# RMS norms by token sums, small roots and a spread by TensorE, early table loads, and a new order in the first head

## What is computed

```python
def rmsnorm(x, g):                      # first block: EPS 1e-6
    xf = x.astype(jnp.float32)
    y = xf * lax.rsqrt(jnp.mean(xf * xf, axis=-1, keepdims=True) + RMS_EPS)
    return (y * g.astype(jnp.float32)).astype(x.dtype)
...
for l in range(DEPTH):                  # DEPTH = 2
    h = h + hybrid_mixer(rmsnorm(h, norm_mix[l]), ...)
    h = h + expert_choice_ffn(rmsnorm(h, norm_ffn[l]), ...)
return rmsnorm(h, norm_final)
...
x = x + sincos_2d(x.shape[1])           # second block
sh1, sc1, gt1, sh2, sc2, gt2 = adaln(c, ada_w[l], ada_b[l])
hx = modulate(rms_norm(x, norm1_g[l]), sh1, sc1)
x_mix = token_mixer(hx @ w_in[l], ...)  # its readout norms each head's 128 values
x = x + gt1 * x_mix
x = x + gt2 * hier_moe(modulate(rms_norm(x, norm2_g[l]), sh2, sc2), ...)
return rms_norm(x, final_norm_g)
```

## Time and profile before

| | |
|---|---|
| three runs | 2255.35, 2257.14, 2259.73 us; median 2257.14 |
| profiled execution | 2259.7 us; its span in the profile 2257.8 us |
| TensorE matmul busy | 1972.8 us, 87% of the span |
| TensorE weight loads busy | 1197.8 us, 53% |
| VectorE busy | 660.3 us, 29% |
| ScalarE busy | 553.7 us, 25% |
| DMA | 748.76 MB, 332 GB/s over the span |

### The profile page before, as it was taken

The page is one execution under the profiler, slowest core; times in us unless marked ns, Lnnn a source line. Parts: engine busy times, 40 slices in busy tenths (PEclk is TensorE's granted clock), DMA queues, the critical chain, the costliest instruction groups (busy, mean ns, idle before and its releaser), DMA issues.

```text
span 2257.8 us, 29187 instructions
## 1 busy us (share of the span) xinstructions
PE 1972.8 (87%) x12802; PEld 1197.8 (53%) x12802; DVE 660.3 (29%) x1074; ACT 553.7 (25%) x849; POOL 0.2 (0%) x4
## 2 busy tenths in 40 slices
PE   7989998777787999998798889879999998888886
PEld 7978943122131897893333434338989843333332
DVE  3477510000000447750150111036657400000001
ACT  3457300000000346630021221023444311010101
POOL 0000000000000000000000000000000000000000
PEclk9999999999999999998999999999999999999999
DMA  9722789999999963378999999983423899999996
GB/s 362 269 105 95 310 356 422 421 421 422 421 421 420 367 241 115 122 310 354 421 418 413 400 418 417 421 327 113 149 94 129 363 422 422 422 422 422 422 422 274
DMA packets 153247, 748.76 MB, mean 332 GB/s; under 512 B 6064, under 2 KB 18608, under 8 KB 78768
## 3 DMA queue, kind: packets, MB, share of 16 engines
q1 hardware_dynamic: 153136, 747.11, 82.4%
HBM read 746.04 MB, written 1.05 MB: 331 GB/s over the span
## 4 chain that ended last, share of the span: by engine, by line
PE 55%; DMA 33%; DVE 5%; ACT 4%; SPq 2%; issue 1%; DVEq 0%; ACTq 0%
PE bank L724 19%; DMA ring<-w_expert_up 11%; DMA ring<-w_expert_down 11%; PE bank L790 9%; DMA ring<-moe_w_down 6%; PE bank L820 5%; PE bank L752 5%; PE bank L727 5%; DMA arena<-moe_w_down 4%; PE bank L831 3%; SPq L2808 2%; PE bank L974 1%; PE bank L994 1%; PE bank L735 1%; PE bank L1041 1%
## 5 line engine op out<-in xcount | busy, mean ns | idle before, releaser
L790 PE MATMUL bank<-ring,arena 128*32 128x512 f32 x2560 | 484.0, 599 | 81.9 <-DMA ring<-w_expert_up 49.3
L820 PE MATMUL bank<-ring,arena 128*32 128x512 f32 x1280 | 286.5, 608 | 80.7 <-DMA ring<-w_expert_down 60.7
L790 PEld LDWEIGHTS bank<-ring,arena 128*32 128x32 f32 x2560 | 122.4, 110 | 400.2 <-issue 255.8
L724 PE MATMUL bank<-arena_parts,ring_parts 128*128 128x256 f32 x1376 | 314.3, 283 | 2.3 <-DVE ring_parts L2453 1.6
L724 PEld LDWEIGHTS bank<-arena_parts,ring_parts 128*128 128x128 f32 x1376 | 233.4, 189 | 11.7 <-issue 3.1
L820 PEld LDWEIGHTS bank<-ring,arena 128*32 128x32 f32 x1280 | 67.9, 111 | 287.9 <-issue 155.1
L1519 ACT ACTIVATE arena<-bank 128x512 f32<-128x512 f32 (+1 forms) x150 | 76.0, 536 | 515.5 <-PE bank L806 241.1
L2035 DVE TENSOR_TENSOR arena<-arena,bank 128x512 f32<-128x512 f32 x24 | 15.8, 685 | 594.4 <-PE bank L790 594.4
L724 PE MATMUL bank<-ring_parts 128*128 128x256 f32 x768 | 153.7, 290 | 10.0 <-DVE ring_parts L2453 5.3
L724 PE MATMUL bank<-hnT_parts,ring_parts 128*128 128x256 f32 x544 | 155.3, 285 | 0.0
L752 PEld LDWEIGHTS bank<-arena 128*128 128x128 f32 x512 | 124.6, 334 | 20.8 <-issue 20.5
(11 more groups left out here) (353 smaller groups left out, 2362.1 us busy)
## 6 DMA issues: line engine op xcount, KB each, us to landing
ring<-w_expert_down SPq DMA_DIRECT2D x64, 2048.0 KB, 26.1
ring<-w_expert_up SPq DMA_DIRECT2D x60, 2048.0 KB, 23.8
ring<-w_expert_gate SPq DMA_DIRECT2D x56, 2048.0 KB, 23.7
ring<-w_in SPq DMA_DIRECT2D x34, 2048.0 KB, 11.2
ring<-moe_w_up SPq DMA_DIRECT2D x24, 2048.0 KB, 28.8
ring<-moe_w_gate SPq DMA_DIRECT2D x20, 2048.0 KB, 32.4
ring<-moe_w_down SPq DMA_DIRECT2D x16, 2048.0 KB, 32.7
arena<-moe_w_down SPq DMA_DIRECT2D x16, 2048.0 KB, 32.1
```

The source lines that it names most:

```text
L724: last = pe.matmul(out[:, n * S:(n + 1) * S], w[:, k, n * P:(n + 1) * P], x[:, k, :], start=first, stop=final)
L790: last = pe.matmul(banks[bank0 + f][32 * e:32 * e + 32, :], x_slots[:, c, 32 * e:32 * e + 32], w[:, k, i, f * 512:(f + 1) * 512], start=c ...
L820: last = pe.matmul(banks[4 + d][32 * e:32 * e + 32, :], hidT[:, f, 32 * e:32 * e + 32], w[:, k, i, d * 512:(d + 1) * 512], start=f == 0, s ...
```

## The change

- All five wide norms sum token by token like the narrow ones. A new helper `token_sums` holds that loop for all norms; root and inverse are of 128x2.
- TensorE spreads the inverse over the partitions again: `spread_inv` multiplies `t_inv[:, half]`, broadcast to 128x128, with the identity, once for each half of the tokens. VectorE then reads the factor from PSUM in place of SBUF.
- A load of Sqrt's table is written out ahead of the squares of each norm and of the readout's squares (`preload_act_table`), and a load of Exp's table behind the root of "m norm".
- The ones and epsilon are set by VectorE and no longer loaded. TensorE starts with the sum of layer 0 when they are set, and waits for the constants only ahead of the first spread.
- In layer 0 ScalarE's high(0) and high(1) come behind the four "hn1 high" copies, and VectorE's low(0) behind the last "hn1 low".
- `HEAD_ORDER` and `ADA_WITH` move each ada unit one unit later in layer 0, and ada unit 1 of layer 1 ahead of unit 1's jobs.

```diff
-HEAD_ORDER = [0, 18, 19, 1, 2, 20, 3, 21] + list(range(4, 18)) + [22, 23]
+HEAD_ORDER = [0, 18, 1, 19, 2, 20, 3, 21] + list(range(4, 18)) + [22, 23]
-ADA_WITH = ({0: (0,), 1: (1,), 2: (2,), 3: (3,)}, {0: (0, 1), 2: (2,), 3: (3,)})
+ADA_WITH = ({1: (0,), 2: (1,), 3: (2,), 4: (3,)}, {0: (0,), 1: (1,), 2: (2,), 3: (3,)})
...
-            def sum_squares_part(step, sq, j, out, prior):
+            def token_sums(step, sq, j, out, prior, **back):
 
-                pe.wait_ge(act_done, act_at(f"{prior} {j}", loops))
+                pe.wait_ge(act_done, act_at(f"{prior} {j}", loops, **back))
                 for k in (2 * j, 2 * j + 1):
-                    last = pe.matmul(out[:, 0:S], ones, sq[:, k, :], start=k == 0, stop=k == DC - 1)
+                    for half in range(TH):
+                        last = pe.matmul(out[:, half:half + 1], sq[:, k, row_of(half)], ones[:, 0:1],
+                                         start=k == 0 and half == 0, stop=k == DC - 1, skip_group_check=True)
                 if j == 3:
                     last.then_inc(pe_done, pe_p.mark(step + " sum"))
+
+            def spread_inv(step, out, **back):
+
+                pe.wait_ge(dve_done, dve_at(f"{step} inv", loops, **back))
+                for half in range(TH):
+                    last = pe.matmul(out[:, row_of(half)], t_inv[:, half:half + 1].broadcast_to([P, P]), ident,
+                                     start=True, stop=True)
+                last.then_inc(pe_done, pe_p.mark(f"{step} spread"))
...
-            pe.wait_ge(consts_loaded, 16)
+            pe.wait_ge(dve_done, dve_at("ones"))
...
                 for j in range(4):
-                    sum_squares_part("norm1", squares, j, norm_bank, "squares")
+                    token_sums("norm1", squares, j, norm_bank, "squares")
+                if not layer:
+                    pe.wait_ge(consts_loaded, 16)
+                spread_inv("norm1", take(5, "dve", "hn1 3"))
...
             norm_bank = take(7, "act", "x norm root")
             for j in range(4):
-                sum_squares_part("x norm", hn3, j, norm_bank, "x squares")
+                token_sums("x norm", hn3, j, norm_bank, "x squares")
+            spread_inv("x norm", take(6, "dve", "x normed 3"))
             idle_products(banks[4], 16)
...
                 if layer:
+                    act.preload_act_table(ACT.Sqrt)
                     high(0)
                 else:
                     act.wait_ge(params_loaded, 16)
-                    act.wait_ge(dve_done, dve_at("c_pad"))
+                    act.wait_ge(dve_done, dve_at("ones"))
                     for r in range(2):
                         act.activation(c_silu[:, :, r], par[:, Q_C + r * DC:Q_C + (r + 1) * DC], ACT.Silu)\
                            .then_inc(act_done, act_p.mark("c_silu"))
+                    act.preload_act_table(ACT.Sqrt)
...
-                act.wait_ge(consts_loaded, 16)
-                root("norm1", bank=banks[6])
-                if not layer:
-                    high(0)
-                high(1)
+                root("norm1", banks[6])
+                if layer:
+                    high(1)
                 for j in range(4):
                     act.wait_ge(dve_done, dve_at(f"hn1 {j}", loops))
                     act.activation(hn_high[:, 2 * j:2 * j + 2, :], hn3[:, 2 * j:2 * j + 2, :], ACT.Copy)\
                        .then_inc(act_done, act_p.mark(f"hn1 high {j}"))
+                if not layer:
+                    high(0)
+                    high(1)
...
             for n in range(4, 8):
                 gate_job(n)
+            act.preload_act_table(ACT.Sqrt)
             act.wait_ge(pe_done, pe_at("o 1 1"))
             for half in range(TH):
                 act.activation(o_sq[:, half, :], banks[4 + half][:], ACT.Square)\
...
-            root("m norm", TH, t_root, banks[1])
+            root("m norm", banks[1])
+            act.preload_act_table(ACT.Exp)
...
-            def normed_inv(step):
-                dve.wait_ge(act_done, act_at(step + " root", loops))
-                then(dve.reciprocal(rms_inv, rms_root), step + " inv")
+            def inverse(step, **back):
+
+                dve.wait_ge(act_done, act_at(step + " root", loops, **back))
+                dve.reciprocal(t_inv, t_root).then_inc(dve_done, dve_p.mark(step + " inv"))
+
+            def spread_out(step, bank, **back):
+
+                inverse(step, **back)
+                dve.wait_ge(pe_done, pe_at(step + " spread", loops, **back))
+                return bank[:, 0:S]
...
-            dve.memset(c_pairs, 0.0).then_inc(dve_done, dve_p.mark("c_pad"))
+            dve.memset(ones, 1.0)
+            dve.memset(eps, EPS)
+            dve.memset(c_pairs, 0.0).then_inc(dve_done, dve_p.mark("ones"))
...
                 for j in range(4):
                     for c in (2 * j, 2 * j + 1):
                         last = dve.scalar_tensor_tensor(hn3[:, c, :], h3[:, c, :], par[:, Q_NORM1 + c:Q_NORM1 + c + 1],
-                                                        rms_inv, ALU.mult, ALU.mult)
+                                                        inv, ALU.mult, ALU.mult)
                     last.then_inc(dve_done, dve_p.mark(f"hn1 {j}"))
-                    if not layer and j == 0:
-                        low(0)
                     if j:
                         hn1_low(j - 1)
                 hn1_low(3)
+                if not layer:
+                    low(0)
                 low(1)
```

More of the change, by code:

```diff
@@ L1138, in router_part @@
                     chunks_ = [(k, half) for k in (2 * j, 2 * j + 1) for half in range(TH)]
[L1139 to L1144, removed]
+                    token_sums("norm2", squares_2, j, sums_bank, "squares2")
                     pe.wait_ge(dve_done, dve_at(f"gh {j}", loops))
@@ L1230, in _ @@
             for j in range(4):
-                sum_squares_part("f norm", hn3, j, norm_bank, "f squares")
+                token_sums("f norm", hn3, j, norm_bank, "f squares")
+            spread_inv("f norm", take(5, "dve", "first block 3"))
             norm_bank = take(7, "act", "x norm root")
             for j in range(4):
-                sum_squares_part("x norm", hn3, j, norm_bank, "x squares")
+                token_sums("x norm", hn3, j, norm_bank, "x squares")
+            spread_inv("x norm", take(6, "dve", "x normed 3"))
             idle_products(banks[4], 16)
@@ L1418, in router2_part @@
                 chunks_ = [(k, half) for k in (2 * j, 2 * j + 1) for half in range(TH)]
-                pe.wait_ge(act_done, act_at(f"m squares {j}"))
-                for k, half in chunks_:
-                    last = pe.matmul(sums_bank[:, half:half + 1], sq_moe[:, k, row_of(half)], ones[:, 0:1],
-                                     start=k == 0 and half == 0, stop=k == DC - 1, skip_group_check=True)
-                if j == 3:
-                    last.then_inc(pe_done, pe_p.mark("m norm sum"))
+                token_sums("m norm", sq_moe, j, sums_bank, "m squares")
                 pe.wait_ge(dve_done, dve_at(f"g2 {j}"))
@@ L1506, in _ @@
             for j in range(4):
-                pe.wait_ge(act_done, act_at(f"tile2b squares {j}", loops, **{"pass": 1}))
-                for k in (2 * j, 2 * j + 1):
-                    last = pe.matmul(banks[0][:, 0:S], ones, hn3[:, k, :], start=k == 0, stop=k == DC - 1)
-            last.then_inc(pe_done, pe_p.mark("l norm sum"))
+                token_sums("l norm", hn3, j, banks[0], "tile2b squares", **{"pass": 1})
+            spread_inv("l norm", banks[1], **{"pass": 1})
         @block.scalar
@@ L1788, in _ @@
                     squared("squares2", j, squares_2)
-                root("norm2", TH, t_root, banks[7])
+                root("norm2", banks[7])
                 act.wait_ge(dve_done, dve_at("router bias", loops))
@@ L1830, in _ @@
                 chunk_squared("f squares", j)
-            root("f norm", bank=banks[6])
+            root("f norm", banks[6])
             high2(0)
@@ L1835, in _ @@
                 chunk_squared("x squares", j)
-            root("x norm", bank=banks[7])
+            root("x norm", banks[7])
             for j in range(4):
@@ L1990, in _ @@
             loops["pass"] = passes
-            one_back = {"pass": 1}
-            act.wait_ge(pe_done, pe_at("l norm sum", loops, **one_back))
-            act.activation(rms_root, banks[0][:, 0:S], ACT.Sqrt, bias=eps, scale=1.0 / D)\
-               .then_inc(act_done, act_p.mark("l norm root"))
+            act.preload_act_table(ACT.Sqrt)
+            root("l norm", banks[0], **{"pass": 1})
         @block.vector
@@ L2379, in _ @@
                         low(first + 6 + j)
-                dve.wait_ge(act_done, act_at("norm2 root", loops))
-                then(dve.reciprocal(t_inv, t_root), "norm2 inv")
+                inverse("norm2")
+                dve.wait_ge(dve_done, dve_at("norm2 inv", loops))
                 dve.wait_ge(pe_done, pe_at("router", loops))
@@ L2677, in _ @@
```

(4 more changed lines are left out.)

55 lines of the change are left out of this document (21 added, 34 removed).

## The result

The changed kernel took 2263.19 us (median of 13 runs, 2259.36 to 2266.9) against 2257.81 of the kernel before (13 runs, 2255.35 to 2260.23). The ratio is 1.0024 (95% interval 1.0016 to 1.0031): slower by 0.24%, or 5.4 us, just beyond the 0.2% that can be told from no change. The time lies inside the range that was given, but the likeliest case, +1.55 and no measurable change, did not come: the growth is three and a half times the forecast one. The profiled execution took 2265.32 us around a span of 2263.4.

A forecast was written before the change was run, and what follows sets the result against it. The chain was taken as bound by TensorE (55%) and DMA (33%), changing hands by stage. Terms 2.65 + 0.7 - 2.3 + 1.2 - 0.7 gave +1.55 on the median of 2257.14: 2258.7 us, range 2254 to 2264.

The forecast's parts named there:

- A: Layer 0's head: earlier sum, but first job meets the slow clock and ada units join the chain; +2.65 us.
- B: Layer 1's head: earlier first chunk, but unit 1's ada unit now precedes its jobs; +0.7 us (-0.3 to +1.4).
- C: Second block's start: shorter norm tails, idle products take the slow clock instead of the first projection; -2.3 us (-4.3 to -1.0).
- D: Readout norm: table load ahead of the squares, no longer covered by VectorE's reduction; +1.2 us (0 to 1.28).
- E: Last norm, at the kernel's end: sum as long, tail shorter; -0.7 us.
- One for one: At all five places of the change on the chain, a shift was counted in full at the kernel's end.
- The clock falls early: Rival: clock falls halfway through three sums after dense work (layer 1, first and last norm); +4.0, 2262.7 us; chance 0.14.
- Narrow products hold the clock: Rival: the fall at 276.5 had another cause, so sums keep full clock; -1.75, 2255.4 us; chance 0.12.
- The table is loaded twice: Rival: a load is still placed at the root, in each layer's norm1 and the readout; 2262.5 us; chance 0.04.
- A drain after a preload: Rival: squares wait for a drain after the written load; readout term +1.4, 2260.1 us; chance 0.03.

The follow-up runs named there:

- The wide operand: Changed kernel with 128 columns of ones moving in place of one in all token sums: 2257.36 us, ratio 0.9999; in norm2 of the kernel before: 2256.53 us, 0.9989.

## Why the prediction was right or wrong

**Terms.** Measured as the growth of the shift from profile to profile across each place: A +2.72 (2.65 predicted), B +2.57 (0.7), C -0.44 (-2.3), D +1.40 (1.2), E -0.5 (-0.7). They sum to 5.75 against 1.55. B and C carry 3.7 of the 4.2 missed. That the spans differ by nearly as much, 5.6, is in part luck: between the five places the shift also moved, by -0.83, +0.88, -0.55 and +0.35. The profile of the run without the readout's load, which has the same instructions up to the readout, shows how much one execution differs from another: B is 1.8 there, as the fall came at 748.3 and the sum took 4.76.

**A was right**, in sign, size and place: first job at 23.44 (22.9), slow clock on it 1.88 (2.3), four ada units in the chain. The chunk came at 14.17, not 13.5: I priced the slow record at 0.195 and it was 6.97/32 = 0.218. The row behind the 0.195 holds router products of 16 columns and begins ahead of the fall. The end at 11.75 does not follow either, as 5.3 and 32 records of 0.195 give 11.5, and the tail took 1.97 against 1.75. "One for one" did not hold quite: of 2.72 at the end of the head, 1.89 was left at the last expert result (739.08 to 740.97).

**B failed at the price of the sum.** The +0.7 assumes a fall during the sum, but charges it to the ada unit and the first job alone: the sum itself was taken as 3.5 and took 5.39, which is the 1.9 that B missed. The wide operand in its place made it 3.82, at a clock of 1.00. (The two parts written down, -1.3 and +1.9, also give +0.6 and not +0.7.)

Behind B, and in no term, lies another 1.5: a half-clock stretch within 853 to 860 (0.76 above, 1.00 in the kernel before) in code that the change does not touch. 48 products took 7.38, and 5.86 in the same place before. It does not belong to the change: the run without the readout's load, with the same instructions up to there, has none, and the same 48 products took 5.84. What puts such a stretch where it is stays open.

**C failed at the price of both sums.** For the first I counted a tail shorter by 0.8. It was shorter by 0.46 (1.86 from sum to first chunk in place of 2.32), but the sum took 4.64 in place of 3.47, so the first chunk came 0.7 later and not 0.8 earlier. For the second I had it end "a part of 1.6 and a little behind" the last square. The clock was at half from about 1509 (0.61 over 1508 to 1512, 0.50 from then on), so 32 records at 0.218 took 6.97 and TensorE itself was the limit: less the shift of 5.34 with which this place was reached (1496.84 to 1502.18) the sum ended at 1517.3, 2.2 behind the predicted 1515.1. Of that 1.5 came with the first norm and 0.7 with the slow records. The gain on the first projection was there (270 records in 32.08 against 276 in 34.79), as forecast for the idle products' new place: from the first chunk to the projection's end 1.07 was won, where the forecast has 0.6.

**D was right** and undone by leaving the load out. **E** came out a little small: the sum at full clock as predicted, but the spread took 1.22, since the clock fell right behind the sum.

**The rivals.** *The clock falls early* is what happened in two of the three sums that it named, and with it the total comes to 2262.7, where the median is 2263.19. That they are so near is partly luck: it had 1.35 in each of three sums, and the runs have 1.9, 1.2 and nothing, and the slow second norm and the stretch at 853 besides. I gave it 0.14, since no row fixed when the fall comes. The range held because its upper end was put at this rival and at the highest A. In norm2 24 narrow records behind the last dense product ran at full clock, and I took that as nearly the 32 of a sum. It differs from place to place: by the windows some 16 records did in layer 1 (745.95 to 747.7 at 0.109), some 21 in the second block (1506.63 to 1508.9), all 32 in the last norm. Ahead of layer 1's sum stand products of 512 and 256 columns with idle time of 1.40, 0.76 and 0.35 between them, ahead of norm2's narrow records a projection without a gap. *Narrow products hold the clock* is refuted by the falls in the sums (0.50 from 747.7 on) and by the runs with the wide operand, on both kernels. *The table is loaded twice* is refuted: one load for each root. *A drain after a preload*: the squares start 0.01 after the load ends (1727.35 + 1.28 to 1728.64), in layer 1 high(0) does as well, and D came to 1.40 and not 2.6. ScalarE: Activation LUTs of the Trainium skill, section "What ACT_TABLE_LOAD costs", has about 1380 ns of drain for a switch; no run here shows it in the engine's own sequence.

**What the written loads were for.** I counted the early loads of layers 0 and 1 as part of their gains of 5.1 and 2.2 us and the norm2 loads as nothing. The runs show none of them to be worth anything measurable (1.0008 without all seven, 1.0012 without the readout's): with the constants' wait gone the compiler's own load is hidden.

## What to carry to other kernels

Ask of every stretch in which TensorE runs only tiny products what clock the work behind it will get, and price it from a row in such a place. Here the cheapest mend was to move 128 columns instead of one: it costs 0.1 us per 32 records and saved 5.8 us in the kernel (2263.19 to 2257.36). The ada unit in TensorE's idle gap was free, and it also paid for the slow start of the clock (3.47 in place of 1.88); moved behind the gap it costs its 1.88 in the chain, and the slow start falls on the first job (13.39 in place of 11.50). And one profile is not enough to price a term of a microsecond: half-clock stretches worth 1.4 to 1.5 came and went between profiles in code that no edit had touched. Before writing a table load, look where the compiler's lands: in these rows it was in the way only where a second wait stood ahead of the root, and then it is that wait that should go.

## What the runs showed of the hardware

- TensorE's granted clock fell from 2.4 to 1.2 GHz while the engine was busy 100% of the time with one-column float32 products (746 to 749 after; at 276.5 before, where products of 16 columns stand between them), and stayed at 2.4 with 128 moving columns at nearly the same cadence. TensorE: Matmul & The Clock Gate of the Trainium skill, section "Part 1: The HAM clock gate (the "warmup" mystery)", ties the gate to how busy the engine is; by the busy time of these rows alone one would not have expected the fall.
- A one-column and a 128-column float32 record with a 128x128 stationary operand cost nearly the same: 3.48 and 3.58 us for 32 at full clock. At half clock the records start 0.213 apart with one column (1515.70 to 1522.31 after) and with 128 (1508.77 to 1514.32 with the wide operand, 6.75 in all as the last three ran at full clock).
- A sum of the same 32 records took 3.48, 4.64, 5.39 or 6.97 us in one execution of one kernel; where it took longer, the clock was at half for part or all of it.
